# Banks of their own for the up rows, silu inside the attention, and the last down passes by token quarters, each with its final layer norm

## The chip, the cores and the metric

The kernel runs on one core of one Trainium2 chip. The metric is the device time of one execution in microseconds (us). The engines are TensorE (PE, with PEld for its weight loads), VectorE (DVE), ScalarE (ACT), GpSimd (POOL) and SyncE (SP, which here issues the DMAs). Each runs its own instruction list in order; they meet by semaphores (`wait_ge` and `then_inc`).

## The reference

One layer of a hybrid encoder, 1024 tokens by 1024 channels in float32:

- `h = x @ w_in`, whose columns feed three mixers: a pooling mixer; a state-space mixer (SSD), where `xbc = silu(conv4(xbc))` and the output is gated by `silu(z)`; and stick-breaking attention with 6 heads of 64, in blocks of 128 queries.
- `x1 = LN(alpha*x + concat(mixers) @ w_out)`.
- `up = conv3(x1 @ w_up)` with 2 x 2816 columns, `ffn = (silu(gate) * val) @ w_down`.
- `out = LN(alpha*x1 + ffn + sigmoid(x1 @ w_gate) * (p @ w_proj))`.

## The kernel before, in words

Everything is float32; products that matter for accuracy are made of three float32r matmuls: high x high, high x low and low x high, where a high part is the value rounded by ScalarE (`hi`, `op_hi`, `h_high`) and the low part the difference, taken by VectorE (`lo`, `op_lo`, `h_low`). Activations lie channels by tokens, in 8 tiles of 128 channels. The 8 PSUM banks of 128 x 512 float32 are shared out by hand. All orders are written out by hand, one list for each engine.

**Attention stage.** A grid of 92 ticks (`NTICK + LAG`) interleaves on all engines the attention of three head pairs (scores, two sigmoids on ScalarE, a scan and a multiplication on VectorE, transposes, a copy `weights_t` by ScalarE, the products with v) with the remaining input projection. `BY_STEP` spreads the pieces of the projection over the ticks. For seven tiles of the SSD input (`x0` to `C1`) the 4-tap conv is done here: `CONV_AT` is the tick of ScalarE's first tap into `cv`, `TAPS_AT` those of VectorE's three further taps (L1562). The tile with dt goes through exp and ln at tick 68 (L1208 to L1213). In the last tick ScalarE waits for the conv and does the silu of `x0`, `x1`, `x2` (L1218 to L1221), then all engines meet at a barrier (`meet`, L451). GpSimd has nothing to do in this stage.

**SSD.** After the barrier TensorE transposes the x and B tiles (`xt`, `bt`, L804) while ScalarE does the silu of B, C and z (L1230 to L1238). VectorE makes `x_dt`, copies the attention's output and runs the states (L1635, L1636); GpSimd makes `x_weighted`, the pooling sums and low parts of the attention output.

**FFN.** Eleven chunks (c = 0 to 10) of two up tiles pairs (pp = 0 even, 1 odd), each with a gate row (r = 0) and a value row (r = 1) of 128 x 1024. A pair of rows is computed by one level of a Strassen-like scheme: seven products (`A11, S1, S2, S3, A12, S4, A22`) of 12 matmuls with 512 columns each (L1009 to L1011), joined by five `combine` steps on VectorE (L1791 to L1801). Row r of tile pp lies in two PSUM banks (`up_row`): `X_BANK = (4, 2)` for r = 0 and `Y_BANK = 0` for r = 1 of both tiles. So the next tile's S2 and S3 may start only when the row before is read: `row_done` is counted by VectorE's second tap (L1767). A row is read by ScalarE's tap (L1343) and two VectorE taps (L1764, L1767); then silu, `glu` (L1774), and h in high and low parts.

The down product of chunk c - 1 runs as 16 `down` steps of 6 matmuls (L667 to L669) between `even` and `even_last` of chunk c. Each writes one of `DOWN_BANKS = (6, 7, 2, 3)` and is added to `acc` by `add_down` (L1816); down k waits for the addition of down k - 3 - 1. The loop order on TensorE is `even(c)`, 16 downs, `even_last(c)`, `odd(c)`. The weights of the down product come through one raw buffer `down_raw`, two loads at a time: D0A with D1A, then D0B with D1B, each after the low part before (L617).

**The end.** In the last chunk all 14 products are made first, then 16 downs for the first tile pair (pp = 0, which are chunk 9's h), then 16 for pp = 1 (the last chunk's h), ordered by halves of the tokens (`h = k // 8`). After half of the tokens is complete, `turn_back(m)` transposes token tile m back between downs; four tiles follow after the last down. A tile's norm: statistics on VectorE (L1701 to L1704), square root on ScalarE (L1462), reciprocal and product (L1949, L1950), normalisation on ScalarE (L1466), gain and bias on GpSimd (L2064, L2065) or, for the tiles in `GAIN_ON_VECTOR`, gain on VectorE (L1939), the last one's bias too (L1955); then a store.

Of the kernel before, what the change touches and what calls it, by code (L numbers as in the profile page):

```python
# [26 lines left out]
P = 128  # L27
D = 1024
S = 1024
HALF = 512  # L30
# [171 lines left out]

CONV_AT, TAPS_AT = [], []
# [6 lines left out]
GAIN_ON_VECTOR = (3, 5, 6, 7)  # L210
# [10 lines left out]
X_BANK, Y_BANK = (4, 2), 0  # L221
DOWN_BANKS = (6, 7, 2, 3)
# [50 lines left out]
def build(nc, ctx, a, out):  # L273
# [95 lines left out]
    h2l = [over("last_h_lo%d" % i, [P, S], (22, 24)[i], F32R) for i in range(2)]  # L369
    pu = over("partial", [P, 2, HALF], 8)  # L370
# [22 lines left out]
    def param(name, i=0, n=1):  # L393
# [21 lines left out]
    tap_done, conv_done, silu_done = sem("tap_done"), sem("conv_done"), sem("silu_done")  # L415
# [156 lines left out]
    def _(eng):  # L572
# [89 lines left out]
    def _(eng):  # L662
# [319 lines left out]
        def first_up(t):  # L982

            n = FFN0 + t
            dst, slot = up_row(t // 2, t % 2), RING_OF[n] % RINGS
            if t == 1:
                eng.wait_ge(sig_done, KT)
            elif t == 2:
                eng.wait_ge(u_free, 2 * KT)
            elif t == 3:  # L990
                eng.wait_ge(row_done, 2)
                column_tile(dst, slot, n, (1,)).then_inc(n1_read, 1)
            column_tile(dst, slot, n, (0,) if t == 3 else (0, 1)).then_inc(u_full, 1)

        def product(c, o, pp, it=0):

            first, second = slice(0, HALF), slice(HALF, S)
            x, y = X_BANK[pp], Y_BANK
# [15 lines left out]
        def down(c, k, pp, it=0):  # L1014

            j, h = (k // 2, k % 2) if pp == 0 else (k % 8, k // 8)
            s_, jc = slice(h * HALF, (h + 1) * HALF), slice(j % 4 * P, (j % 4 + 1) * P)
            if k == 0:
                eng.wait_ge(h_done, 2 * (c + pp) + 2 * it)
            if (pp == 0 and k % 8 == 0) or (pp == 1 and k in (0, 4)):  # L1020
                eng.wait_ge(op_lo_done, lo_count(c, D1A if j < 4 else D1B, pp) + 18 * it)
            first = 16 * (c - 1 + pp)
            if k >= 4 or pp:
                eng.wait_ge(dn_added, first + k - 3 + 16 * it)
            bank = 4 + k % 4 if c == LASTC else DOWN_BANKS[k % 4]
            h_h, h_l = (h2h, h2l) if pp else (hh, hl)
            for i in range(2):
                o = ((D0A, D1A), (D0B, D1B))[j // 4][i]
                last = three(ps[:, bank, :], op_place(c, o, pp, False)[:, jc], op_place(c, o, pp, True)[:, jc],
                             h_h[i][:, s_], h_l[i][:, s_], i == 0, i == 1)  # L1030
            last.then_inc(dn_full, 1)

        def even(c, it=0):
# [4 lines left out]
            eng.wait_ge(row_done, 4 * (c - 1) + 4 + 4 * it)  # L1038
# [16 lines left out]
        def odd(c, it=0):  # L1055
# [9 lines left out]
            eng.wait_ge(row_done, 4 * c + 2 + 4 * it)  # L1065
# [9 lines left out]
        def chunk(c, it=0):  # L1075

            even(c, it)
            for k in range(16):
                if k == 2:
                    eng.wait_ge(row_done, 4 * (c - 1) + 3 + 4 * it)  # L1080
                down(c, k, 0, it)
# [3 lines left out]
        def turn_back(m):  # L1085

            if m in (0, MT // 2):
                eng.wait_ge(dn_added, 16 * (CHUNKS - 1) + 8 + 8 * (m // 4))
# [4 lines left out]
            for kt in range(KT):  # L1093
                last = turn(two(m % 2)[:, kt * P:(kt + 1) * P], acc[:, kt, m * P:(m + 1) * P])
# [11 lines left out]
        eng.wait_ge(row_done, 4 * LASTC + 1)  # L1106
        for k in range(16):
            down(LASTC, k, 0)
        for k in range(16):
            if k in (9, 10, 12, 13):  # L1110
                turn_back((9, 10, 12, 13).index(k))
            down(LASTC, k, 1)
        for m in range(MT // 2, MT):
# [4 lines left out]
    def _(eng):  # L1118
# [57 lines left out]
        for n in range(NTICK + LAG):  # L1176
# [23 lines left out]
            if n in CONV_AT:  # L1200
# [3 lines left out]
                if j:  # L1204
                    eng.wait_ge(conv_done, j)
                act(cv[:, j, :], ht[:, j, :], ACT.Identity, scale=param("conv_w", 4 * j + 3),
                    bias=param("conv_b", j)).then_inc(tap_done, 1)
            if n == DT_AT + 1:  # L1208
# [9 lines left out]
            if n == NTICK + LAG - 1:  # L1218
                eng.wait_ge(conv_done, 7)
                for j in range(3):  # L1220
                    act(cv[:, j, :], cv[:, j, :], ACT.Silu).then_inc(silu_done, 1)  # L1221
# [8 lines left out]
        for j in (3, 4):  # L1230
            act(cv[:, j, :], cv[:, j, :], ACT.Silu).then_inc(silu_done, 1)
# [3 lines left out]
        for j in (5, 6):  # L1235
            act(cv[:, j, :], cv[:, j, :], ACT.Silu).then_inc(silu_done, 1)
        for j in range(3):
            act(ht[:, 7 + j, :], ht[:, 7 + j, :], ACT.Silu).then_inc(silu_done, 1)  # L1238
# [18 lines left out]
        nc.scalar.preload_act_table_set("natural_log_exp_and_others")  # L1257
# [198 lines left out]
        h_high(c, 1)  # L1456
        op_hi(c, D0B, 1)
        op_hi(c, D1B, 1)

        for m in range(MT):  # L1460
            eng.wait_ge(o_eps, m + 1)
            act(st[:, m, 15:16], st[:, m, 14:15], ACT.Sqrt).then_inc(o_sqrt, 1)  # L1462
            eng.wait_ge(o_aff, m + 1)
            if m >= 4:
                eng.wait_ge(stored[m % 4], 16 * (m // 4))
            act(on[:, m % 4, :], two(m % 2), ACT.Identity, scale=st[:, m, 13:14],  # L1466
# [4 lines left out]
    def _(eng):  # L1471
# [310 lines left out]
        def combine(c, pp, step, it=0):  # L1782

            n = 10 * (c - 1) + 5 * pp
            x, y = X_BANK[pp], Y_BANK
# [18 lines left out]
        def add_down(c, pp, ks, it=0):  # L1804

            first = 16 * (c - 1 + pp)
            for k in ks:
                j, h = (k // 2, k % 2) if pp == 0 else (k % 8, k // 8)
# [6 lines left out]
                bank = 4 + k % 4 if c == LASTC else DOWN_BANKS[k % 4]  # L1815
                v.tensor_tensor(dst, dst, ps[:, bank, :], ALU.add).then_inc(dn_added, 1)  # L1816
# [28 lines left out]
        def chunk(c, it=0):  # L1845
# [13 lines left out]
            add_down(c, 0, range(8, 16), it)  # L1859
# [72 lines left out]
        add_down(c, 1, range(9))  # L1932
# [4 lines left out]
        def gain(m):  # L1937
            eng.wait_ge(o_nrm, m + 1)
            v.tensor_tensor(on[:, m % 4, :], on[:, m % 4, :], lng[:, :], ALU.mult).then_inc(o_gain, 1)  # L1939

        for m in range(MT):
            eng.wait_ge(o_full, m + 1)
            statistics(m, two(m % 2)).then_inc(o_eps, 1)
            if m < 4:
                add_down(c, 1, ((9,), (10, 11), (12, 13), (14, 15))[m])
            if m - 1 in GAIN_ON_VECTOR:
                gain(m - 1)
            eng.wait_ge(o_sqrt, m + 1)
            link(v.reciprocal(st[:, m, 13:14], st[:, m, 15:16]))  # L1949
            v.scalar_tensor_tensor(out=st[:, m, 12:13], in0=st[:, m, 12:13], scalar=-1.0, in1=st[:, m, 13:14],  # L1950
                                   op0=ALU.mult, op1=ALU.mult).then_inc(o_aff, 1)
        m = MT - 1
        gain(m)
        eng.wait_ge(o_gain, len(GAIN_ON_VECTOR))
        v.tensor_tensor(on[:, m % 4, :], on[:, m % 4, :], lnb[:, :], ALU.add).then_inc(o_last, 1)  # L1955
# [3 lines left out]
    def _(eng):  # L1959
# [16 lines left out]

        meet(eng, 1)
# [165 lines left out]
```

## Time and profile before

| | us |
|---|---|
| median of 3 runs (1435.45 to 1437.79) | 1437.26 |
| the profiled execution | 1435.54 |
| its span in the trace | 1433.8 |
| TensorE busy | 1320.9 (92%) |
| VectorE busy | 879.5 (61%) |
| ScalarE busy | 507.4 (35%) |
| GpSimd busy | 208.1 (15%) |

The span runs from the first to the last instruction. Matmuls are drawn 0.40 us long, but they overlap: the next begins before one has ended, so TensorE's busy time leaves the pipeline's fill out. In a timeline row the bracket at the end gives the time that the engine stood idle before it and who released it. A row with x2 or more is several like instructions drawn as one, from the first one's start to the last one's end.

### The profile page before, as it was taken

Reading aid. Unit: us, or ns where it says so; the run is one execution under the profiler, and the core shown is the slowest. Engines: PE = TensorE matmul, PEld = TensorE weight load, DVE = VectorE, ACT = ScalarE, POOL = GpSimd, SP = SyncE. Lnnn points to the kernel's source line nnn. Section 1 sums busy time; section 2 is a strip of 40 time slices with the busy share of each in tenths; the row PEclk is TensorE's granted clock in tenths of the full one; section 3 lists DMA queues with packets and bytes.
Section 4 is the critical chain, followed back from the end, with each engine's and each line's share of the span. In section 5 each row is a group of like instructions: output and inputs, shape, how many; then the busy total and the mean of one; then the engine's idle time right before and its main releaser. Section 6 shows DMA issues by size and latency. Waiting matters only on the chain.

```text
span 1433.8 us, 16333 instructions
## 1 busy us (share of the span) xinstructions
PE 1320.9 (92%) x6084; PEld 1057.1 (74%) x6084; DVE 879.5 (61%) x1060; ACT 507.4 (35%) x747; POOL 208.1 (15%) x141
## 2 busy tenths in 40 slices
PE   7999999899767999999999999999999999999993
PEld 5787788677655788788877777777777777777772
DVE  3536646534387845532467676767676776767778
ACT  4445445444544224312333232423232332323412
POOL 0000000000271000510012111111122021111116
PEclk9999999899988999999999999999999999999996
DMA  5101000000001311310020111102010101111102
GB/s 217 52 23 45 30 30 30 30 30 15 1 1 59 103 44 60 102 45 30 30 74 30 60 44 44 59 31 83 32 59 29 59 29 59 44 45 59 59 16 117
DMA packets 22947, 71.93 MB, mean 50 GB/s; under 512 B 2544, under 2 KB 2800, under 8 KB 22896
## 3 DMA queue, kind: packets, MB, share of 16 engines
q1 hardware_dynamic: 22896, 71.22, 14.6%
q8 instruction: 36, 0.59, 0.2%
q14 instruction: 15, 0.12, 0.0%
HBM read 67.02 MB, written 4.19 MB: 50 GB/s over the span
## 4 chain that ended last, share of the span: by engine, by line
PE 59%; DVE 18%; ACT 5%; issue 5%; DMA 1%; ACTq 1%; POOL 1%; DVEq 0%; SPq 0%; POOLq 0%
PE ps L667 12%; PE ps L669 12%; PE ps L668 12%; PE ps L1009 5%; PE ps L1011 5%; PE ps L1010 5%; DVE conv_ff L1764 4%; DVE conv_ff L1767 2%; PE ps L761 2%; ACT conv_ff L1343 2%; DVE w_lo L553 1%; PE ps L721 1%; PE ps L745 1%; PE ps L804 1%; ACT w_hi L548 1%
## 5 line engine op out<-in xcount | busy, mean ns | idle before, releaser
L1816 DVE TENSOR_TENSOR acc<-acc,ps 128x512 f32<-128x512 f32 x176 | 117.6, 685 | 71.2 <-PE ps L669 71.2
L667 PE MATMUL ps<-x_hi,w_hi 128*128 128x512 f32 x336 | 142.0, 423 | 14.1 <-DVE x_lo L502 10.5
L667 PE MATMUL ps<-h_hi,w_hi 128*128 128x512 f32 x320 | 127.6, 399 | 11.3 <-DVE acc L1816 11.3
L668 PE MATMUL ps<-x_lo,w_hi 128*128 128x512 f32 x336 | 134.6, 400 | 0.0
L669 PE MATMUL ps<-x_hi,w_lo 128*128 128x512 f32 x336 | 134.2, 399 | 0.0
L669 PE MATMUL ps<-h_hi,w_lo 128*128 128x512 f32 x320 | 126.6, 396 | 0.0
L668 PE MATMUL ps<-h_lo,w_hi 128*128 128x512 f32 x320 | 126.6, 396 | 0.0
L1009 PE MATMUL ps<-mix_hi,w_hi 128*128 128x512 f32 x320 | 126.6, 396 | 0.0
L1010 PE MATMUL ps<-mix_lo,w_hi 128*128 128x512 f32 x320 | 126.6, 396 | 0.0
L1011 PE MATMUL ps<-mix_hi,w_lo 128*128 128x512 f32 x320 | 126.6, 396 | 0.0
L1009 PE MATMUL ps<-t_hi,w_hi 128*128 128x512 f32 x240 | 96.8, 403 | 18.2 <-DVE conv_ff L1767 18.2
L2039 POOL TENSOR_TENSOR weight_sums<-raw 128x512 f32<-128x512 f32 x20 | 30.4, 1518 | 495.4 <-DMA raw<-u_up 470.3
L548 ACT ACTIVATE w_hi<-weight_sums 128x512 fp32r<-128x512 f32 x40 | 25.3, 632 | 214.2 <-PE ps L669 170.9
L1011 PE MATMUL ps<-t_hi,w_lo 128*128 128x512 f32 x240 | 94.9, 396 | 0.0
L1010 PE MATMUL ps<-t_lo,w_hi 128*128 128x512 f32 x240 | 94.9, 395 | 0.0
L1343 ACT ACTIVATE conv_ff<-ps,params 128x1024 f32<-128x1024 f32 x44 | 53.1, 1206 | 103.6 <-DVE ps L1801 42.5
L1531 DVE TENSOR_TENSOR_SCAN ps<-ps,zero 128x1024 f32<-128x1024 f32 (+7 forms) x48 | 65.3, 1361 | 37.6 <-ACT ps L1167 37.5
L667 PEld LDWEIGHTS ps<-x_hi,w_hi 128*128 128x128 f32 x336 | 64.5, 192 | 28.5 <-DVE x_lo L502 10.5
L667 PEld LDWEIGHTS ps<-h_hi,w_hi 128*128 128x128 f32 x320 | 60.1, 188 | 29.7 <-DVE acc L1816 15.6
L667 PE MATMUL ps<-mix_hi,w_hi 128*128 128x512 f32 x192 | 76.9, 400 | 3.7 <-DVE mix_lo L1710 3.7
L1764 DVE SCALAR_TENSOR_TENSOR conv_ff<-ps,params,conv_ff 128x1023 f32<-128x1023 f32 x44 | 56.3, 1280 | 35.8 <-ACT conv_ff L1343 35.6
L1187 ACT ACTIVATE weights_t<-ps 128x512 f32<-128x512 f32 (+1 forms) x60 | 33.3, 555 | 122.9 <-PE ps L745 122.8
(240 smaller groups left out, 2847.9 us busy)
## 6 DMA issues: line engine op xcount, KB each, us to landing
raw<-u_up SPq DMA_DIRECT2D x44, 512.0 KB, 3.3
raw<-u_in SPq DMA_DIRECT2D x22, 512.0 KB, 3.3
down_raw<-u_down SPq DMA_DIRECT2D x44, 256.0 KB, 2.8
x_stage<-u_x SPq DMA_DIRECT2D x8, 512.0 KB, 7.7
raw<-u_out SPq DMA_DIRECT2D x8, 512.0 KB, 3.2
x_nat<-x_nat SPq DMA_DIRECT2D x8, 512.0 KB, 3.3
raw<-u_gate SPq DMA_DIRECT2D x8, 512.0 KB, 3.3
out<-o_norm SPq DMA_DIRECT2D x8, 512.0 KB, 2.6
```

The lines of the kernel that those rows point to most:

```text
L548: nc.scalar.activation(op_place(c, o, pp, False), op_raw(o), ACT.Copy).then_inc(op_hi_done, 1)
L667: mm(dst, w_hi, x_hi, start=first, stop=False)
L668: mm(dst, w_hi, x_lo, start=False, stop=False)
L669: return mm(dst, w_lo, x_hi, start=False, stop=last)
L1009: mm(dst, w_h[:, k], t_h[:, kt, :], start=fresh and kt == 0, stop=False, skip_group_check=True)
L1010: mm(dst, w_h[:, k], t_l[:, kt, :], start=False, stop=False, skip_group_check=True)
L1011: last = mm(dst, w_l[:, k], t_h[:, kt, :], start=False, stop=kt == 3, skip_group_check=True)
L1187: act(pair(un[:, :]), pair(ps[:, 6, :]), ACT.Copy).then_inc(wt_out, 1)
L1343: act(cf[:, r, :], up_row(pp, r), ACT.Identity, scale=column(w, 12, it), bias=column(b, 4, it)).then_inc(row_tap, 1)
L1531: link(v.tensor_tensor_scan(z[:, ::-1], z[:, ::-1], zero[:, 0:1].broadcast_to([P, keys]), 1.0, ALU.mult, ALU.add))
L1764: v.scalar_tensor_tensor(out=cf[:, r, 1:], in0=src[:, :S - 1], scalar=column(w + 1, 12, it), in1=cf[:, r, 1:], op0=ALU.mult, op1=ALU.add). ...
L1816: v.tensor_tensor(dst, dst, ps[:, bank, :], ALU.add).then_inc(dn_added, 1)
```

## The change

- `Y_BANK` becomes `(0, 6)`: row 1 of the odd tile goes to banks 6 and 7. The waits of S2 move: even S2 waits for `row_done` 4(c-1) + 2, odd S2 for none (in the last chunk for the chunk before); down 0 waits for the odd tile's row 1.
- In a chunk VectorE does the taps and five down additions before `op_lo(A11, 1)`.
- In the attention, three taps after a conv tile's start, ScalarE takes the sigmoid of the conv (`GATE_AT`) and GpSimd multiplies it on; the z tiles follow the same way. The ten silus on ScalarE go. A tile's first tap waits for the silu of the one before, and comes at the earliest 3 ticks (`GATE_LAG`) after its last tap.
- The last down passes: four quarters of 256 tokens; matmuls have 256 columns instead of 512, all four terms (two pp, two i) accumulate in one bank, which holds two channel tiles (`LAST_BANKS`), and VectorE adds once for both. In the first quarter the terms go in three phases by when h is ready. Each later quarter carries the transposes of two tiles of the quarter before. Weights D0B, D1B of pp = 1 get places of their own.
- Norm: reciprocal and a `tensor_scalar` instead of `scalar_tensor_tensor`; tiles 0 to 5 by ScalarE and GpSimd, tiles 6 and 7 by two `scalar_tensor_tensor` on VectorE.

```diff
-    CONV_AT.append(max([evacuated_at(("tile", _name)) + 1] + [t[-1] + 1 for t in TAPS_AT[-1:]]))
+    CONV_AT.append(max([evacuated_at(("tile", _name)) + 1] + [t[-1] + GATE_LAG for t in TAPS_AT[-1:]]))
+GATE_AT = [t[-1] + 1 for t in TAPS_AT]
+for _name in H_TILES[7:10]:
+    GATE_AT.append(max(evacuated_at(("tile", _name)) + 1, GATE_AT[-1] + 2))
-X_BANK, Y_BANK = (4, 2), 0
-DOWN_BANKS = (6, 7, 2, 3)
+X_BANK, Y_BANK = (4, 2), (0, 6)
+DOWN_BANKS, LAST_BANKS = (6, 7, 2, 3), (4, 5, 0, 1)
...
+        def last_down(q, jp, k):
+            pp, i = divmod(k, 2)
+            h_h, h_l = (h2h, h2l) if pp else (hh, hl)
+            s_ = slice(q * QUARTER, (q + 1) * QUARTER)
+            for j in (2 * jp, 2 * jp + 1):
+                o = ((D0A, D1A), (D0B, D1B))[j // 4][i]
+                w_h, w_l = op_place(LASTC, o, pp, False), op_place(LASTC, o, pp, True)
+                jc = slice(j % 4 * P, (j % 4 + 1) * P)
+                dst = ps[:, LAST_BANKS[jp], j % 2 * QUARTER:(j % 2 + 1) * QUARTER]
+                mm(dst, w_h[:, jc], h_h[i][:, s_], start=k == 0 and j % 2 == 0, stop=False, skip_group_check=True)
+                mm(dst, w_h[:, jc], h_l[i][:, s_], start=False, stop=False, skip_group_check=True)
+                last = mm(dst, w_l[:, jc], h_h[i][:, s_], start=False, stop=k == 3, skip_group_check=True)
+            if k == 3:
+                last.then_inc(dn_full, 1)
...
-            eng.wait_ge(row_done, 4 * (c - 1) + 4 + 4 * it)
+            eng.wait_ge(row_done, 4 * (c - 1) + 2 + 4 * it)
...
-            eng.wait_ge(row_done, 4 * c + 2 + 4 * it)
+            if c == LASTC:
+                eng.wait_ge(row_done, 4 * (c - 1) + 4)
...
-                if k == 2:
-                    eng.wait_ge(row_done, 4 * (c - 1) + 3 + 4 * it)
+                if k == 0:
+                    eng.wait_ge(row_done, 4 * (c - 1) + 4 + 4 * it)
...
+        for jp in range(4):
+            if jp in (0, 2):
+                eng.wait_ge(op_lo_done, lo_count(LASTC, D1B if jp else D1A, 0))
+            last_down(0, jp, 0)
+            last_down(0, jp, 1)
+        eng.wait_ge(h_done, 2 * LASTC + 1)
+        for jp in range(4):
+            if jp in (0, 2):
+                eng.wait_ge(op_lo_done, lo_count(LASTC, D1B if jp else D1A, 1))
+            last_down(0, jp, 2)
+        eng.wait_ge(h_done, 2 * LASTC + 2)
+        for jp in range(4):
+            last_down(0, jp, 3)
+        for q in range(1, 4):
+            for jp in range(4):
+                eng.wait_ge(dn_added, 16 * (LASTC - 1) + 4 * (q - 1) + jp + 1)
+                for k in range(4):
+                    last_down(q, jp, k)
+                if jp in (0, 2):
+                    turn_back(2 * q - 2 + jp // 2)
+        for m in range(MT - 2, MT):
+            turn_back(m)
...
+            if n in GATE_AT:
+                j = GATE_AT.index(n)
+                if j < 7:
+                    eng.wait_ge(conv_done, j + 1)
+                    act(ht[:, j, :], cv[:, j, :], ACT.Sigmoid).then_inc(gate_done, 1)
+                else:
+                    for hh_ in range(2):
+                        wait_evacuated(eng, PLACE[(H_TILES[j], hh_)])
+                    eng.wait_ge(silu_done, j)
+                    act(ht[:, 6, :], ht[:, j, :], ACT.Sigmoid).then_inc(gate_done, 1)
...
             combine(c, 0, 4, it)
+            taps(c, 0, 0, it)
+            add_down(c, range(5), it)
             op_lo(c, A11, 1, it)
-            taps(c, 0, 0, it)
-            add_down(c, 0, range(8), it)
+            add_down(c, range(5, 8), it)
...
-        add_down(c, 0, range(0, 2))
-        taps(c, 1, 1)
         op_lo(c, D0A, 1)
         op_lo(c, D1A, 1)
-        add_down(c, 0, range(2, 6))
+        taps(c, 1, 1)
         glu(c, 1)
-        add_down(c, 0, range(6, 9))
-        h_low(c, 1)
-        add_down(c, 0, range(9, 11))
         op_lo(c, D0B, 1)
         op_lo(c, D1B, 1)
-        add_down(c, 0, range(11, 16))
-        add_down(c, 1, range(9))
+        h_low(c, 1)
+        add_last(0, range(4))
...
+        for j in range(10):
+            eng.wait_ge(gate_done, j + 1)
+            x = cv[:, j, :] if j < 7 else ht[:, j, :]
+            g.tensor_tensor(x, x, ht[:, min(j, 6), :], ALU.mult).then_inc(silu_done, 1)
```

## Rows read from the trace of the kernel before

**Rows 1.** The page, part 1: busy us, share of the span, instructions.

```profile
PE 1320.9 (92%) x6084; PEld 1057.1 (74%) x6084; DVE 879.5 (61%) x1060; ACT 507.4 (35%) x747; POOL 208.1 (15%) x141
```

**Rows 2.** Waits of TensorE: us in total, times, longest.

```profile
PE ps L1009 <- DVE conv_ff L1767: 18.2, 19, 1.9
...
PE ps L667 <- DVE acc L1816: 11.3, 10, 1.2
```

**Rows 3.** Timeline of TensorE, one loop chunk: start, us, instruction, count, [idle before].

```profile
943.00 0.50 PE L667 MATMUL ps<-h_hi,w_hi 128*128 128x512 f32 x1 [1.19 <-DVE acc L1816]
...
968.99 0.49 PE L1009 MATMUL ps<-t_hi,w_hi 128*128 128x512 f32 x1 [0.52 <-DVE conv_ff L1767]
969.32 0.39 PE L1010 MATMUL ps<-t_lo,w_hi 128*128 128x512 f32 x1
...
990.38 0.49 PE L1009 MATMUL ps<-t_hi,w_hi 128*128 128x512 f32 x1 [1.54 <-DVE conv_ff L1767]
```

**Rows 4.** Timeline of all engines around the barrier after the attention.

```profile
375.18 0.60 ACT L1136 ACTIVATE h_tiles<-ps 128x512 f32<-128x512 f32 x1 [0.64 <-PE ps L669]
...
380.18 7.07 PE L804 MATMUL ps<-tables,conv 128*128 128x128 f32 x40 [5.04 <-ACTq L451]
...
396.63 7.79 POOL L2006 TENSOR_TENSOR mix_lo<-sb_out,mix_hi 128x1024 fp32r<-128x1024 f32 x3
```

**Rows 5.** Timeline of the end, and the window around the stall at 576.84.

```profile
1352.85 0.40 PE L667 MATMUL ps<-h_hi,w_hi 128*128 128x512 f32 x1
...
1354.74 1.28 DVE L553 TENSOR_TENSOR w_lo<-down_raw,w_hi 128x512 fp32r<-128x512 f32 x2
...
1359.33 1.16 ACT L548 ACTIVATE w_hi<-down_raw 128x512 fp32r<-128x512 f32 x2 [1.46 <-DMA down_raw<-u_down]
...
1402.77 0.40 PE L669 MATMUL ps<-last_h_hi,w_lo 128*128 128x512 f32 x1
...
1406.08 0.68 DVE L1701 BATCH_NORM_STATS2 ln_stats<-ps 128x6 f32<-128x512 f32 x1
...
1407.71 1.93 DVE L1939 TENSOR_TENSOR o_norm<-o_norm,ln_gain 128x1024 f32<-128x1024 f32 x1
...
1429.41 1.22 DVE L1955 TENSOR_TENSOR o_norm<-o_norm,ln_bias 128x1024 f32<-128x1024 f32 x1
...
core 0: us, PE busy (x) PEld busy (x) DVE busy (x) ACT busy (x) POOL busy (x), PEclk, DMA share, GB/s
576.00:580.50 4.50, 3.66 (x10) 2.93 (x11) 4.50 (x3) 1.72 (x2) 4.42 (x3) 0.62 0.29 88
```

**Rows 6.** Timeline of VectorE in the same loop chunk and the next.

```profile
942.26 1.87 DVE L1816 TENSOR_TENSOR acc<-acc,ps 128x512 f32<-128x512 f32 x3
...
998.18 0.69 DVE L553 TENSOR_TENSOR w_lo<-down_raw,w_hi 128x512 fp32r<-128x512 f32 x1
...
1001.88 0.70 DVE L1799 TENSOR_TENSOR ps<-partial,ps 128x512 f32<-128x512 f32 x1 [1.44 <-PE ps L1011]
...
1005.27 1.28 DVE L1764 SCALAR_TENSOR_TENSOR conv_ff<-ps,params,conv_ff 128x1023 f32<-128x1023 f32 x1
...
1007.90 1.27 DVE L1816 TENSOR_TENSOR acc<-acc,ps 128x512 f32<-128x512 f32 x2
```

**Rows 7.** Timeline of ScalarE, the tap behind combine 4.

```profile
1002.91 1.21 ACT L1343 ACTIVATE conv_ff<-ps,params 128x1024 f32<-128x1024 f32 x1 [3.19 <-DVE ps L1799]
```

**Rows 8.** Timeline of the attention around tick 68.

```profile
286.24 1.26 ACT L1206 ACTIVATE conv<-h_tiles,params 128x1024 f32<-128x1024 f32 x1
...
303.42 0.92 PE L761 MATMUL ps<-weights_t,v_natural 128*128 128x256 f32 x3 [0.82 <-ACT weights_t L1187]
```

**Rows 9.** Timeline of short matmuls; the page's group of weight loads (busy, mean ns).

```profile
73.80 0.28 PE L721 MATMUL ps<-k_hi,q_hi 64*128 64x256 f32 x2
73.91 0.27 PE L721 MATMUL ps<-k_lo,q_hi 64*128 64x256 f32 x2
...
428.33 3.84 PE L860 MATMUL ps<-tables,small 128*128 128x128 f32 x32
...
L667 PEld LDWEIGHTS ps<-h_hi,w_hi 128*128 128x128 f32 x320 | 60.1, 188 | 29.7 <-DVE acc L1816 15.6
```

More of the change, by code:

```diff
@@ L508, in op_place @@
     def op_place(c, o, pp, lo):
+        if c == LASTC and pp and o in (D0B, D1B):
+            return (last_l if lo else last_h)[:, (D0B, D1B).index(o), :]
         s_ = (position(c, o, pp) + 4) % 6
@@ L533, in wait_op_place @@
         q = position(c, o, pp) - 6
+        if c == LASTC and pp and o in (D0B, D1B):
+            eng.wait_ge(prod_full, product_count(c, S2, 1))
+            return
         if c == 1 and q < 0:
@@ L1012, in product, with down @@
             last.then_inc(prod_full, 1)
-        def down(c, k, pp, it=0):
-            j, h = (k // 2, k % 2) if pp == 0 else (k % 8, k // 8)
+        def down(c, k, it=0):
+            j, h = k // 2, k % 2
             s_, jc = slice(h * HALF, (h + 1) * HALF), slice(j % 4 * P, (j % 4 + 1) * P)
             if k == 0:
[L1019 to L1026, printed above, removed]
+                eng.wait_ge(h_done, 2 * c + 2 * it)
+            if k % 8 == 0:
+                eng.wait_ge(op_lo_done, lo_count(c, D1A if j < 4 else D1B, 0) + 18 * it)
+            if k >= 4:
+                eng.wait_ge(dn_added, 16 * (c - 1) + k - 3 + 16 * it)
@@ L1105, in _ @@
         odd(LASTC)
[L1106 to L1113, printed above, removed]
+        eng.wait_ge(row_done, 4 * LASTC + 2)
+        eng.wait_ge(h_done, 2 * LASTC)
+        for jp in range(4):
[19 more added lines that the diff above has]
+        for m in range(MT - 2, MT):
             turn_back(m)
@@ L1228, in task @@
             return two(pair), d_free[pair]
-        for j in (3, 4):
-            act(cv[:, j, :], cv[:, j, :], ACT.Silu).then_inc(silu_done, 1)
+        nc.scalar.preload_act_table_set("natural_log_exp_and_others")
         for g in range(2):
@@ L1941, in _, with rows, affine @@
[L1941 to L1947, printed above, removed]
+        def rows(m):
+            return two((1, 3)[m % 2])
+        def affine(m):
             eng.wait_ge(o_sqrt, m + 1)
             link(v.reciprocal(st[:, m, 13:14], st[:, m, 15:16]))
-            v.scalar_tensor_tensor(out=st[:, m, 12:13], in0=st[:, m, 12:13], scalar=-1.0, in1=st[:, m, 13:14],
-                                   op0=ALU.mult, op1=ALU.mult).then_inc(o_aff, 1)
@@ L1952, in _ @@
[L1952 to L1955, printed above, removed]
+            v.tensor_scalar(st[:, m, 12:13], st[:, m, 12:13], st[:, m, 13:14], -1.0, ALU.mult,
+                            ALU.mult).then_inc(o_aff, 1)
+        for q in range(1, 4):
+            m = 2 * q - 2
+            add_last(q, (0,))
+            eng.wait_ge(o_full, m + 1)
+            statistics(m, rows(m)).then_inc(o_eps, 1)
+            add_last(q, (1,))
+            affine(m)
+            add_last(q, (2,))
+            eng.wait_ge(o_full, m + 2)
+            statistics(m + 1, rows(m + 1)).then_inc(o_eps, 1)
+            add_last(q, (3,))
+            affine(m + 1)
@@ new lines, in _ @@
+        for m in range(MT - 2, MT):
+            eng.wait_ge(o_full, m + 1)
+            statistics(m, rows(m)).then_inc(o_eps, 1)
+            eng.wait_ge(stored[m % 4], 16)
+            y = on[:, m % 4, :]
+            v.scalar_tensor_tensor(out=y, in0=rows(m), scalar=st[:, m, 12:13], in1=lng[:, :], op0=ALU.subtract,
+                                   op1=ALU.mult).then_inc(o_cent, 1)
+            eng.wait_ge(o_sqrt, m + 1)
+            link(v.reciprocal(st[:, m, 13:14], st[:, m, 15:16]))
+            eng.wait_ge(o_cent, m - MT + 3)
+            v.scalar_tensor_tensor(out=y, in0=y, scalar=st[:, m, 13:14], in1=lnb[:, :], op0=ALU.mult,
+                                   op1=ALU.add).then_inc(o_last, 1)
```

86 lines of the change are left out of this document (41 added, 45 removed).

## The prediction

> **What bounds the kernel now.** I read the page first, for busy shares: TensorE works 1320.9 of 1433.8 us and nothing else comes near [rows 1], so time can only leave in TensorE's idle stretches or at the ends, where it has nothing to do. Next the waits of TensorE: two of its largest are 18.2 us for the second tap of an up row, in 19 waits, and 11.3 us for the additions of down results, in 10 [rows 2]. The timeline of one loop chunk shows where they stand: before down 4 (943.00), before S2 of the odd tile (968.99) and before S2 of the even tile of the next chunk (990.38) [rows 3]. Last the two ends that the diff touches: from 375.14 to 380.18 TensorE waits for ScalarE, which loads a table and does three silus [rows 4]; and after the last down matmul at 1402.77 the program runs to 1433.8, 31 us of layer norm of the last tiles [rows 5].
>
> What one stall costs: idle plus restart. A matmul is drawn 0.40 long, the next one starts 0.233 after it, and only the second one after a stall comes 0.33 later (968.99 to 969.32) [rows 3]. So a stall costs its idle time + 0.17 + 0.10 = idle + 0.27. The 0.233: from 968.99 to 990.38 are 84 matmuls (seven products of 12), less 1.54 + 0.27 for the stall at the end: 19.58 / 84. A product is 2.8.
>
> **Chunks.** Row 1 of the odd tile gets banks 6 and 7 of its own. Both S2 products then wait for a row that has long been read, so all 19 stalls go: 18.2 + 19 x 0.27 = 23.3 [rows 2, 3]. Three of these waits come back at other places. Down 0 now waits for the odd tile's second tap (done by 990.38, wanted at 999): nothing. A11 and S1 of the odd tile write banks 2 and 3 as before. S2 of the odd tile writes bank 7, freed by down 13, which S1's wait for down 15 already covers: nothing.
>
> What is late next? The vector chain. The odd tile starts two products and a stall before 968.99, at 968.99 - 5.6 - 0.69 = 962.7 [rows 3]; from there to the downs TensorE has 13 products, 36.4, to 999.1. VectorE in that stretch does not wait for TensorE up to the low part of D1B at 998.18 [rows 6]; that and the low part of A22 are 0.69 each, so combine 4, which until now waited for TensorE until 1001.88, starts at about 999.5. From there the rows give: activation 1.03 after it (1002.91) [rows 7], 1.21 long, taps 0.15 later, two taps and the start of the additions 2.63 after (1005.27 to 1007.90) [rows 6], and the first addition releases down 4 after 0.74 (942.26 to 943.00) [rows 3, 6]. That is 999.5 + 1.03 + 1.21 + 0.15 + 2.63 + 0.74 = 1005.3. Down 4 is ready at 999.1 + 24 x 0.233 = 1004.7. So a stall of 0.6, 0.75 with its restart, is left where 1.19 + 0.27 = 1.46 is now. The low part of A11, moved from before the taps to behind five additions, is what keeps the taps at 1005.27 today, where the activation ends at 1004.12; in its new place it falls between additions that wait for TensorE, and its reader comes after all the downs: nothing. Nine chunks have this stall: 11.3 less the one in the last tile (0.9), plus 9 x 0.27, is 12.8; 9 x 0.75 = 6.8 stays; 6.0 goes. Chunks together: **-29.3**. Bounds: if the down stall stays whole, -23.3; if it vanishes, -36.
>
> **Silu in the attention.** ScalarE gets 10 sigmoids of 1.05 and loses 10 silus; GpSimd gets 10 multiplications of 128x1024, 2.6 each by the nearest row (three in 7.79) [rows 4]. No sigmoid adds a table load: the scores use the same function. The ScalarE queue behind a sigmoid holds the copies of transposed weights, which TensorE wants only a tick later. One place has no slack: the tap of tile C1 (1.26, at 286.24) moves from two ticks earlier into the tick with the softplus and its table loads, whose end TensorE already waits for (303.42) [rows 8]: +1.3. GpSimd's multiplications hold up VectorE where it reads two operands from SBUF: a gain multiplication begun at 1407.71 beside GpSimd took 1.93 instead of 1.22 [rows 5]. Only taps and low parts are of that kind in the attention; TensorE has little idle there, so nearly all is covered. I take +0.7 (bounds 0, and 10 x 0.7 = 7). Sum **+2.0**.
>
> **Between attention and scan.** The last evacuation ends at 375.78; the barrier can let TensorE go at 375.95 instead of 380.18 [rows 4]: -4.2. The 40 transposes behind it start at half clock after an idle of 5.04: they take 7.07, 0.18 each, where 32 matmuls of the same width take 3.84, 0.12 each, at full clock [rows 4, 9]. After an idle of under 1 us the clock should stay up; 34 of them stand before VectorE's last x dt: about 6.4 becomes 3.7, -2.7 (bounds 0 and -2.7). The later silus (C, z) stood beside VectorE's copies and states, which set the pace: 0. Sum **-6.9**.
>
> **The tail.** Call T the start of the downs (1352.85) [rows 5]. Now: T + 50.3 to the end of the downs, T + 81.0 to the end.
>
> 192 matmuls of 512 columns become 384 of 256. Their spacing is the greatest unknown. Rows: score matmuls of 256 columns follow at 0.11 to 0.12 (73.80, 73.91), though two share the array by rows; full 128x128 loads with a 128-column matmul each follow at 0.12 on average (3.84 / 32), without the first one's latency 0.11 [rows 9]. Half of 0.233 is 0.117: I take it, and 384 x 0.117 = 192 x 0.233 = 44.8, no change. Upper bound: a load is drawn 0.188 long [rows 9]; at that spacing 72.2, +27.4.
>
> Now the first quarter, which has too little work to cover the second tile's h. (1) k = 0, 1: 48 matmuls, 5.6; at half of it TensorE waits for the low part of D1B,0, ending at T + 3.2 (1354.74 + 1.28): end T + 6.1. (2) k = 2 needs D0A,1 and D1A,1: they land at T + 6.5 (1359.33) [rows 5], high 0.62, low 0.68 and 0.6: T + 8.5, a stall of 2.4. Its second half needs D1B,1, whose load is issued only then (one raw buffer): landing 3.3 later as between 1356.02 and 1359.33, T + 11.8; high parts, low parts behind glu: T + 13.9. TensorE stood from T + 9.9, a stall of 4.0. End T + 15.4. (3) k = 3 needs h low, behind taps, glu, the low parts and ScalarE's high copy: T + 15.5. End T + 18.3.
>
> Each further quarter: 96 x 0.117 = 11.2, and two tiles of 8 transposes, 0.9 + 0.1 each: 13.2. Downs end at T + 18.3 + 39.6 = T + 57.9, 7.6 later than now. Four additions of 0.69 and two tiles' statistics and scalars (2.0 each) take VectorE 6.8 of each 13.2, two tiles' gain and bias GpSimd 4 x 2.6 = 10.4: covered.
>
> Behind it: last add and transposes 2.2; statistics 1.6 (1406.08 to 1407.71) [rows 5]; centring with gain 1.3, reciprocal 0.2, scale with bias 1.2; and this once more, 4.3 each; the store's 3.2 (from 1430.63 to the end, 1433.8) [rows 5]: 14.0. Tile 5's bias on GpSimd (2.6) lies over tile 6's last step, which reads SBUF twice: up to +2. End T + 57.9 + 16 = T + 73.9: -7.0. But two stalls of 2.4 and 4.0 may halve the clock: after an idle of 3.65 the granted clock of 576 to 580.5 was 0.62 [rows 5], a loss of some 1.5; I add 1.0. Sum **-6.0**, bounds -11 and 0 without the spacing.
>
> **Sum.** -29.3 + 2.0 - 6.9 - 6.0 = -40.2 on the profiled execution's 1435.5 (span 1433.8): 1395.3. The median of the timed runs, 1437.3, is 1.7 above; so 1397.
>
> **Rivals.** (a) Weight loads bind the short matmuls (0.15 to 0.19 apart). For: loads are drawn 0.188 long, and each begins when the matmul before begins. Against: 0.11 with 128 columns, where loads are drawn as long. 1397 + 27 = 1424; from 0.15, 1410. Chance 6%. (b) Loads don't overlap at all with a matmul on the same rows: 0.188 + 0.117 = 0.305, 384 x 0.305 = 117, +72: 1469, **slower**; it turns into a loss from (44.8 + 40.2) / 384 = 0.22. Against: then 512 columns would be 0.40 apart, not 0.233. Chance 2%. By the Trainium skill ("TensorE: Matmul & The Clock Gate", Part 3, The mechanism), LDWEIGHTS overlaps with in-flight matmuls only when the row group differs; by that rule (b) would hold, and the trace's 0.233 and 0.11 speak against it. (c) GpSimd's products and late gates hold VectorE or ScalarE in the attention: ten waits for a whole multiplication, 26 at most, 1405 to 1421. For: ScalarE already lets TensorE wait there [rows 8]. Chance 8%. (d) The chunk change does less than it says: VectorE's chain is nearer than I counted and gives the stalls back at down 4 or at S4, half of 29: 1411. For: combine 4 has no slack left. Against: VectorE is idle 39% [rows 1]. Chance 12%. The forecast: 72%.
>
> **Numbers.** Own range of the forecast 1390 to 1405; with (c), (d) and part of (a): 1389 to 1411. A measurement here tells 0.2% from no change. Faster by more: 0.95 (all but (b) and what I have not thought of), within 0.2% 0.02, slower 0.03.
>
> **What would show it.** Right: no wait on L1767's taps before S2; a stall under 1 us at down 4; transposes 0.11 apart after the barrier, some 4 us earlier; 256-column matmuls 0.117 apart; in the first quarter two stalls of 2 to 4 us; the end 16 us behind the last down. Wrong: a spacing over 0.13, attention more than 5 us longer, or chunks over 63 us (14 products, 96 matmuls of downs and the stall are 39.2 + 22.4 + 0.75 = 62.4).

## The result, and the profile after

| | median us | runs | ratio to before, 95% interval |
|---|---|---|---|
| before | 1436.36 | 4 (1433.75 to 1437.79) | |
| changed | 1392.76 | 4 (1391.88 to 1394.17) | 0.9699 [0.9682, 0.9717] |

The forecast was 1397 (1389 to 1411). The profiled execution of the changed kernel took 1391.88, its span is 1389.8. The page, part 1, as in [rows 1]: TensorE has 192 matmuls more (the last downs have 256 columns) and 9.6 us less busy time; GpSimd has the ten products.

```profile
PE 1311.3 (94%) x6276; PEld 1064.6 (77%) x6276; DVE 860.7 (62%) x1041; ACT 502.4 (36%) x744; POOL 233.2 (17%) x152
```

Waits of TensorE after (us in total, times, longest), to be held against [rows 2]: the wait for the second tap of an up row is gone, that for the down additions has shrunk to 1.5; the one for the transposed weights of the attention has grown from 0.8 to 1.9 (L771); and new ones stand before the last downs (L1049).

```profile
PE ps L1049 <- DVE last_w_lo L563: 5.7, 1, 5.7
...
PE ps L1049 <- DVE w_lo L563: 2.7, 2, 2.5
...
PE ps L771 <- ACT weights_t L1225: 1.9, 1, 1.9
...
PE ps L677 <- DVE acc L1855: 1.5, 7, 0.2
```

Timeline after: the wait behind the softplus tick, as in [rows 8], and TensorE's restart behind the barrier with VectorE's first states operation, as in [rows 4].

```profile
303.59 1.13 PE L771 MATMUL ps<-weights_t,v_natural 128*128 128x256 f32 x4 [1.95 <-ACT weights_t L1225]
...
376.22 4.59 PE L814 MATMUL ps<-tables,conv 128*128 128x128 f32 x40 [0.72 <-ACTq L456]
...
385.65 0.55 DVE L1675 TENSOR_TENSOR states<-states,small 128x384 f32<-128x384 f32 x1
```

The end, TensorE, as in [rows 5]. T, the start of the last downs, is 1312.17:

```profile
1312.17 0.28 PE L1049 MATMUL ps<-h_hi,w_hi 128*128 128x256 f32 x1
...
1315.39 0.39 PE L1049 MATMUL ps<-h_hi,w_hi 128*128 128x256 f32 x1 [0.22 <-DVE w_lo L563]
...
1320.94 0.36 PE L1049 MATMUL ps<-last_h_hi,w_hi 128*128 128x256 f32 x1 [2.45 <-DVE w_lo L563]
...
1328.26 0.58 PE L1049 MATMUL ps<-last_h_hi,last_w_hi 128*128 128x256 f32 x1 [5.67 <-DVE last_w_lo L563]
...
1373.94 0.28 PE L1051 MATMUL ps<-last_h_hi,last_w_lo 128*128 128x256 f32 x1
```

Three anchors cut both spans into parts: the last projection matmul before the barrier (374.75 before, 375.10 after), the restart before the FFN (576.84; 568.81), and T (1352.85; 1312.17).

| part | before | after | change | forecast |
|---|---|---|---|---|
| start to barrier | 374.75 | 375.10 | +0.35 | +2.0 |
| barrier, scan, output projection | 202.09 | 193.71 | -8.4 | -6.9 |
| FFN up to T | 776.01 | 743.36 | -32.65 | -29.3 |
| T to the end | 80.95 | 77.6 | -3.3 | -6.0 |

(The attention started 0.6 earlier in this execution, at 60.94 instead of 61.56, so its own part is +0.97.) The measured median is 4.2 below the forecast. In the table the gains that I had set too low (attention, barrier, chunks: 1.7 + 1.5 + 3.3) outweigh the one that I had set too high (the end, 2.7); that errors of both signs met is luck.

### The profile page after: what moved, and what is told of

Read it like the earlier page. It is cut to its first block, busy times and chain, and to the rows that moved or that the text cites. A ratio compares the mean times of both kernels' runs of the same rounds, so it can differ in the third digit from the quotient of the medians.

```text
span 1389.8 us, 16699 instructions
## 1 busy us (share of the span) xinstructions
PE 1311.3 (94%) x6276; PEld 1064.6 (77%) x6276; DVE 860.7 (62%) x1041; ACT 502.4 (36%) x744; POOL 233.2 (17%) x152
## 4 chain that ended last, share of the span: by engine, by line
PE 68%; DVE 12%; ACT 4%; issue 3%; DMA 2%; DVEq 0%; SPq 0%; ACTq 0%
PE ps L677 12%; PE ps L679 12%; PE ps L678 12%; PE ps L1020 7%; PE ps L1018 7%; PE ps L1019 7%; PE ps L771 2%; DMA down_raw<-u_down 2%; DVE conv_ff L1804 1%; ACT conv_ff L1381 1%; PE ps L731 1%; PE ps L755 1%; PE ps L814 1%; DVE w_lo L563 1%; PE ps L1049 1%
## 5 line engine op out<-in xcount | busy, mean ns | idle before, releaser
L1855 DVE TENSOR_TENSOR acc<-acc,ps 128x512 f32<-128x512 f32 x144 | 96.1, 685 | 53.4 <-PE ps L679 52.9
L1019 PE MATMUL ps<-mix_lo,w_hi 128*128 128x512 f32 x320 | 126.6, 396 | 0.0
L1020 PE MATMUL ps<-mix_hi,w_lo 128*128 128x512 f32 x320 | 126.6, 396 | 0.0
L677 PE MATMUL ps<-h_hi,w_hi 128*128 128x512 f32 x288 | 114.6, 398 | 1.5 <-DVE acc L1855 1.5
L679 PE MATMUL ps<-h_hi,w_lo 128*128 128x512 f32 x288 | 113.9, 396 | 0.0
L678 PE MATMUL ps<-h_lo,w_hi 128*128 128x512 f32 x288 | 113.9, 395 | 0.0
L679 PE MATMUL ps<-mix_hi,w_lo 128*128 128x512 f32 x192 | 76.4, 398 | 0.0
L678 PE MATMUL ps<-mix_lo,w_hi 128*128 128x512 f32 x192 | 76.4, 398 | 0.0
```

The costliest lines, as they stand in the source:

```text
L677: mm(dst, w_hi, x_hi, start=first, stop=False)
L678: mm(dst, w_hi, x_lo, start=False, stop=False)
L679: return mm(dst, w_lo, x_hi, start=False, stop=last)
L1019: mm(dst, w_h[:, k], t_l[:, kt, :], start=False, stop=False, skip_group_check=True)
L1020: last = mm(dst, w_l[:, k], t_h[:, kt, :], start=False, stop=kt == 3, skip_group_check=True)
L1855: v.tensor_tensor(dst, dst, ps[:, DOWN_BANKS[k % 4], :], ALU.add).then_inc(dn_added, 1)
```

## Experiments

Nine kernels, called by their numbers below (kernel 4 is that of experiment 4). The first four ran beside the kernel before at 1435.74 us (median of 11 runs), the next four beside it at 1435.36, the last at 1434.95.

**1. The banks alone.** Kernel before with the second bank pair, its waits and VectorE's order in the chunk.

```diff
-X_BANK, Y_BANK = (4, 2), 0
+X_BANK, Y_BANK = (4, 2), (0, 6)
...
-            op_lo(c, A11, 1, it)
             taps(c, 0, 0, it)
-            add_down(c, 0, range(8), it)
+            add_down(c, 0, range(5), it)
+            op_lo(c, A11, 1, it)
+            add_down(c, 0, range(5, 8), it)
```

> Kernel before with the second bank pair for row 1 of the odd tile, its waits and VectorE's new order in the chunk; attention and the end as before (downs of the last chunk in banks 4, 5, 0, 1, the transposes back in 2, 3, 6, 7). Theory: all of the 32.7 us by which the stretch from TensorE's restart before the FFN to the first last down is shorter in the changed kernel comes from this part: 32 to 33 less than before, about 1404; no wait for L1767's taps, the downs' stall 0.2 idle. Rival, the prediction's count: 29.3 less, 1407. Rival: some of it came only with the new end, because the last chunk's VectorE order is another: 23 to 27 less.

Measured: 1403.19, ratio 0.9771 [0.9758, 0.9784], 32.5 less. Its waits for down additions come to this, from 11.3 in [rows 2]; none is left for the up row's tap:

```profile
PE ps L667 <- DVE acc L1816: 2.4, 8, 0.9
```

From the restart before the FFN to T it takes 743.7, the changed kernel 743.4. So the whole gain of the FFN stretch is this edit's; the new end has no part in it.

**2. Silu in the attention alone.** The `GATE_AT`, ScalarE and GpSimd hunks on the kernel before.

> Kernel before with the silus moved into the attention, nothing else. Theory from the two traces: -4.3 of waiting at the barrier, -2.7 because the 40 transposes run at the full granted clock, about -1.5 behind them, +1.0 in the attention: 7 to 8.5 less than before, about 1428.5. Rival, the prediction's sum: GpSimd's products cost the attention 2.0 and nothing is gained behind the transposes: 4.9 less, 1431.5.

Measured: 1428.77, ratio 0.9955 [0.9941, 0.9969], 7.0 less (4.5 to 8.5 by the interval). The median stands at the lower end of the theory's 7 to 8.5, and the interval doesn't exclude the prediction's 4.9; the trace is plainer than the total. TensorE's 40 transposes start after 0.72 instead of 5.04 and take 4.59 instead of 7.07 [rows 4]:

```profile
378.00 4.59 PE L808 MATMUL ps<-tables,conv 128*128 128x128 f32 x40 [0.72 <-ACTq L455]
```

**3. Both, with the old end.**

> The two parts above together, the end as before. Theory: they add, and the new end is worth 3.3 in the changed kernel: this one takes 3.3 more than the changed kernel, about 1396. Rival: the new end is worth the predicted 6.0 and the rest less: 1399. Rival: the parts share stalls and don't add: more than 1400.

Measured: 1396.91, ratio 0.9726 [0.9714, 0.9739]. 38.8 less, where the two parts alone give 39.5: they add. The changed kernel at 0.9699 is 0.0027 lower, about 4 us, the intervals just meeting; by the traces the end is worth 3.3 (T to the end 81.0 in this kernel, 77.6 in the changed one).

**4. Why the end gave so little: raw buffers of their own.** Changed kernel; D0B and D1B of both tiles load early into two places (the norm's gain and bias follow into them later), so no down load waits for another's low part. The edit also changes two orders in the last chunk: each of ScalarE's two taps of the last tile stands behind the high copies that it was ahead of, the silu behind the second tap, and VectorE takes the first tile's low parts of D0B and D1B before combine 4. What it gives belongs to the places and the orders together.

```diff
+    dn_own = [over("down_own%d" % i, [P, 2, HALF], 11 + i) for i in range(2)]
...
+        for pp in range(2):
+            for i in range(2):
+                eng.dma_start(dn_own[pp][:, i, :], a["u_down"][2 * (LASTC - 1 + pp) + i][:, HALF:D]
+                              ).then_inc(own_in[pp], 16)
```

> Changed kernel, with raw buffers of their own for the weights D0B, D1B of both tiles in the last chunk (loaded as soon as the slots are free; the norm's gain and bias come into the same slots afterwards), so that no down load waits for another's low part. Theory: the stalls of 2.45 and 5.67 us in the first token quarter are a chain of loads through one raw buffer, and the lower clock behind them is theirs too. Left is about 2 us before the second half of k = 2 (low part of D1B behind glu) and under 0.5 before k = 3: first quarter 7 to 8.5 shorter, in all 1385 (1383 to 1387). Rival: h, not the weights, sets the quarter's end (taps, glu and h_low would end at the same time anyway): 2 to 3 less, 1390. Rival: the extra megabyte of loads beside the last products slows VectorE and ScalarE: no gain.

Measured: 1385.60, ratio 0.9651 [0.9638, 0.9663]; T to the end 70.0 instead of 77.6. Of three waits in the first quarter one of 1.79 is left, at the place expected:

```profile
1324.52 0.38 PE L1059 MATMUL ps<-last_h_hi,last_w_hi 128*128 128x256 f32 x1 [1.79 <-DVE last_w_lo L571]
```

In the changed kernel's trace the chain of loads is what the wait of 5.67 hangs on: TensorE waits for VectorE's low part, that for ScalarE's high part, and ScalarE stands 6.26 us for the last load. That the whole 7.6 comes from this chain isn't shown, because of the orders changed with it.

```profile
1318.84 1.15 ACT L558 ACTIVATE w_hi<-down_raw 128x512 fp32r<-128x512 f32 x2 [1.65 <-DMA down_raw<-u_down]
1326.25 1.15 ACT L558 ACTIVATE last_w_hi<-down_raw 128x512 fp32r<-128x512 f32 x2 [6.26 <-DMA down_raw<-u_down]
```

**5. Is it the banks or the order?** Changed kernel with VectorE's old order in the loop (low part of A11, taps, eight additions).

> Changed kernel, but in the loop VectorE takes the low part of A11 of the odd tile before the taps again, as the kernel before did. Theory: the reorder is what took the stall at down 4 from 1.2 to 0.2 idle in each chunk: the taps end 0.6 to 0.7 later, so the stall comes back as 0.7 to 0.9 idle in nine chunks, 5 to 7 us in all, some 1398. Rival: the banks alone did it, because combine 4 no longer waits: stall still 0.2 idle, time as the changed kernel's.

Measured: 1400.72 in one run, and 10.0 us of waits for down additions in 9 (longest 1.3) instead of 1.5 in 7. The kernel before has 10.3 in the same nine chunks: at down 4 the banks alone give next to nothing. The price is more than the theory's 0.7 for each chunk. VectorE in one chunk of this kernel, and of the changed one:

```profile
857.36 0.69 DVE L1839 TENSOR_TENSOR ps<-partial,ps 128x512 f32<-128x512 f32 x1
860.13 0.69 DVE L563 TENSOR_TENSOR w_lo<-raw,w_hi 128x512 fp32r<-128x512 f32 x1 [2.08 <-ACT w_hi L558]
860.74 1.28 DVE L1804 SCALAR_TENSOR_TENSOR conv_ff<-ps,params,conv_ff 128x1023 f32<-128x1023 f32 x1
```

```profile
855.90 0.69 DVE L1839 TENSOR_TENSOR ps<-partial,ps 128x512 f32<-128x512 f32 x1
858.28 1.28 DVE L1804 SCALAR_TENSOR_TENSOR conv_ff<-ps,params,conv_ff 128x1023 f32<-128x1023 f32 x1 [1.69 <-ACT conv_ff L1381]
```

From combine 4 to the tap it is 3.38 against 2.38. The low part itself is 0.6 of that; 0.4 more is its wait for the high part, which ScalarE makes only behind its own tap.

**6. An idle before the transposes.** Changed kernel with four copies on ScalarE ahead of the barrier.

```diff
+        eng.wait_ge(silu_done, 10)
+        for k in range(4):
+            act(ht[:, 6, :], ht[:, 6, :], ACT.Copy).then_inc(pad, 1)
+            eng.wait_ge(pad, k + 1)
         meet(eng, 1)
```

> Changed kernel with four more copies of 128x1024 on ScalarE ahead of the barrier after the attention (they change nothing in the result). Theory: TensorE waits 4.2 to 4.9 us longer there, and the 40 transposes behind it run at the lower clock level again, 0.18 instead of 0.11 apart: up to 2.7 more, so that the first states operation behind them comes 6 to 7.5 later. Rival: the transposes were slow before because of the silus that ran beside them, not because of the idle time ahead: only 4.2 to 4.9 later, transposes 0.11 apart.

Measured: 1398.37 in one run. The transposes begin 4.1 later than in the changed kernel, and run at the lower of the two clock levels first; window rows of this kernel, then of the changed one (us, busy time and count of each engine, PEclk, DMA share, GB/s):

```profile
380.00:384.00 4.00, 3.65 (x18) 3.65 (x19) 1.88 (x4) 1.54 (x2) 1.75 (x3) 0.57 0.00 0
384.00:388.00 4.00, 4.00 (x33) 3.90 (x32) 2.18 (x6) 1.94 (x2) 3.23 (x5) 1.00 0.00 0
```

```profile
376.00:380.00 4.00, 3.78 (x35) 3.78 (x36) 1.95 (x4) 2.75 (x4) 2.48 (x4) 1.00 0.00 0
```

In the first window 18 have begun, in the changed kernel's 35; they take 6.25 in all against 4.59, with no silu beside them in either. The first states operation follows 5.5 later than in the changed kernel (391.18, 385.65), under the 6 expected: the slow part cost 1.4 this time, where the kernel before lost 2.2, because the clock rose sooner. Idle time as the cause is shown, its size varies.

**7. Twice the products on GpSimd.** The second product of each pair changes the result; it took 1.9 to 2.9 us beside the first one's 2.4.

```diff
             g.tensor_tensor(x, x, ht[:, min(j, 6), :], ALU.mult).then_inc(silu_done, 1)
+            eng.wait_ge(silu_done, j + 1)
+            g.tensor_tensor(x, x, x, ALU.mult)
```

> Changed kernel in which GpSimd multiplies each of the ten products in the attention once more by itself (this changes the result). Theory from the trace: GpSimd's products cost VectorE next to nothing there, because VectorE has slack for what they hold up: attention up to 1 us longer. Rival, the prediction's 0.07 for each of ten products (0.7 in all) and its bound (0.7 for each): 0.7 to 7 more, to be seen as longer taps (1.28 alone) with TensorE waiting behind them.

Measured: 1392.13 in one run; from TensorE's matmul at 285 to the transposes 90.9 as in the changed kernel. The twelve taps of the window from 200 to 377 are as long as in the kernel before, 1278 ns (line, busy us, mean ns):

```profile
L1602 DVE SCALAR_TENSOR_TENSOR conv<-h_tiles,params,conv 128x1023 f32<-128x1023 f32 (+2 forms) x12 | 15.3, 1279 | 0.2
```

**8. Filling the first quarter; the end reordered.** On kernel 4.

```diff
-DOWN_BANKS, LAST_BANKS = (6, 7, 2, 3), (4, 5, 0, 1)
+DOWN_BANKS, LAST_BANKS = (6, 7, 2, 3), ((4, 5, 0, 1), (2, 3, 6, 7))
...
+        last_down(0, 0, 2)
+        last_down(0, 1, 2)
+        eng.wait_ge(row_done, 4 * LASTC + 3)
+        for k in range(3):
+            last_down(1, 0, k)
+        eng.wait_ge(op_lo_done, lo_count(LASTC, D0B, 1))
+        last_down(0, 2, 2)
+        last_down(0, 3, 2)
...
                                    op1=ALU.mult).then_inc(o_cent, 1)
+        for m in range(MT - 2, MT):
+            y = on[:, m % 4, :]
             eng.wait_ge(o_sqrt, m + 1)
```

> Changed kernel with the own raw buffers of the run before, and two things more: (1) the quarters take banks 4, 5, 0, 1 and 2, 3, 6, 7 in turn, so that the first three terms of the second quarter's first tile pair stand in the first quarter before its last term, and term k = 2 waits only for the weights that it reads; (2) at the end VectorE centres both last tiles before it scales the first, so that no operation with two SBUF inputs stands beside GpSimd's last one. Theory: (1) takes away the 1.8 us stall in the first quarter and the lower clock behind it (60 matmuls 0.146 apart instead of 0.120, 1.6): 3.4 less; (2) the scaling of tile 6 takes 1.28 instead of 3.27: 1.5 to 2 less. From 1385.6 to 1380.5 (1379.5 to 1382). Rival: the clock falls anyway, at another place: 1382. Rival for (2): the two last stores now follow each other closely and take longer: 0 to 0.5 less from it.

Measured: 1378.99, ratio 0.9604 [0.9588, 0.9620]: 6.6 less than kernel 4, and the fastest with kernel 9. From T (1313.15) to the end 64.6. TensorE waits nowhere in the first quarter and keeps the full clock:

```profile
1313.00:1331.00 18.00, 18.00 (x154) 17.95 (x153) 14.06 (x17) 6.19 (x8) 0.00 (x0) 1.00 0.10 40
```

At the end VectorE centres tile 7 before it scales tile 6. The scaling was held 2 us by GpSimd in the changed kernel:

```profile
1379.01 2.34 POOL L2128 TENSOR_TENSOR o_norm<-o_norm,ln_bias 128x1024 f32<-128x1024 f32 x1
1379.16 3.27 DVE L2016 SCALAR_TENSOR_TENSOR o_norm<-o_norm,ln_stats,ln_bias 128x1024 f32<-128x1024 f32 x1
...
1385.36 1.28 DVE L2016 SCALAR_TENSOR_TENSOR o_norm<-o_norm,ln_stats,ln_bias 128x1024 f32<-128x1024 f32 x1
```

and stands behind it here (POOL's last ends at 1371.2):

```profile
1368.88 2.34 POOL L2148 TENSOR_TENSOR o_norm<-o_norm,ln_bias 128x1024 f32<-128x1024 f32 x1
...
1371.85 1.28 DVE L2036 SCALAR_TENSOR_TENSOR o_norm<-o_norm,ln_stats,ln_bias 128x1024 f32<-128x1024 f32 x1
```

From the last down to the end 13.9 instead of 15.9: the 2.0 in full. From T to the end it is 5.4 less than in kernel 4, and 6.6 lie between the medians; ahead of T the edit changes nothing, so the other 1.2 isn't its doing.

**9. C1's tap two ticks later.** On kernel 8.

> The run before (filled) with the first tap of tile C1 two ticks later, out of the tick in which ScalarE computes softplus with its table loads (the three other taps and the gates behind it follow). Theory: the tap is what lengthens TensorE's wait for the transposed weights from 0.82 to 1.95: the wait goes back to 0.8, and with it the lower clock that followed it in some executions: 1.1 to 2 less, about 1377.6. Rival: the tap only moves the wait, since the ticks behind are as full: same time, a new wait of about 1 us at the later tick. Rival: C1's gate, the last of the seven, now comes too late for z and the barrier: 1 to 3 more.

Measured: 1378.96, ratio 0.9608 [0.9594, 0.9621]: the same as kernel 8. The wait is back at its old length, and no other came:

```profile
302.94 1.13 PE L784 MATMUL ps<-weights_t,v_natural 128*128 128x256 f32 x4 [0.82 <-ACT weights_t L1244]
```

From 285.83 to the transposes it is 89.2, 1.7 less than the changed kernel's 90.9. The rest of the execution took this back (0.5 each before, in the scan stage and behind it), which is what executions differ by. The local gain is shown, one in the median is not.

## Why the prediction was right, step by step

**The pieces of a stall.** Idle + 0.27 held: 19 waits gone are 23.3, the down waits fell from 11.3 + 10 x 0.27 = 14.0 to 1.5 + 7 x 0.27 = 3.4. The 0.9 + 0.27 of the last tile's wait lay behind T before; without it the two sums are 23.3 + 12.8 - 3.4 = 32.7, and 32.65 was measured.

**Down 4: the mis-sized term (6.0, measured 9.4).** The mechanism was right, the moved low part too. I left 0.6 idle in each of nine chunks; it was 0.2 in seven. Combine 4 starts 0.2 behind the first down (855.90 and 855.69), where I had 0.4; and the rest is my own double count: the 0.6 was the delay against the point where the next matmul would have started, so 0.17 of the restart was in it already.

```profile
861.65 0.50 PE L677 MATMUL ps<-h_hi,w_hi 128*128 128x512 f32 x1 [0.20 <-DVE acc L1855]
```

A whole chunk takes 62.1 (first down to first down, 855.69 to 917.76), where I had 62.4.

**Attention (2.0, measured 0.97 in one execution).** The tap in the tick of the softplus costs 1.95 - 0.82 = 1.13, close to the 1.3. The 0.7 for GpSimd was not there: the taps kept their length, VectorE's low parts of this stretch grew from 1225 to 1289 ns, and nothing waited for them; experiment 7 doubles GpSimd's work without effect. The 0.97 is a kind value: from TensorE's restart at 61.56 (60.94 after) to the last projection matmul it took 313.2 before and 314.2 in the changed kernel, but 316.6 and 316.7 in kernels 3 and 4, with the same instructions, so the cost was 1 to 3.5 by the clock's course (last section).

**Barrier (4.2, measured 4.3) and clock (2.7, measured 2.2)** up to the first states operation: 11.65 behind the transposes' start before, 9.43 after. Another 1.8 came behind it, which I had put at 0. Experiment 6 keeps ScalarE free of the silus and still has the idle: from its first states matmul (394.62) to the restart before the FFN it takes 180.7, the kernel before 181.6 (from 395.28), the changed one 179.7. The clock's course was worth little there: over the 26 us behind that matmul kernels 2 and 8 have a granted clock of 0.76 and the changed one 0.86, yet they take 179.9 and the changed one 179.7. The silus of C and z in ScalarE's queue are what the kernel before alone has; but kernel 6 doesn't have them and takes 0.9 more than the changed one, so how the 1.8 divides stays open.

**The tail: the step that was too good (6.0, measured 3.3).** Point by point from T = 1312.17:
- k = 0, 1 end at T + 6.1 by the forecast; the last of its 48 starts at T + 6.05. D1A's low part was put at T + 8.5 and TensorE restarts at T + 8.8.
- D1B's low part was put at T + 13.9, from a landing 3.3 after the low part before. It came 5.45 after (1320.80 to 1326.25), and TensorE restarted at T + 16.1: 2.2 lost. I took one row (1356.02 to 1359.33) as the price of every load of the kind. In the kernel before the next load's landing was hidden, as ScalarE was not waiting for it.
- A wait of 5.67 halved the clock: the next 36 matmuls took 6.44 instead of 4.2, 2.2 lost where I had allowed 1.0.

```profile
1328.00:1331.00 3.00, 2.74 (x13) 2.74 (x14) 1.44 (x2) 1.63 (x2) 0.00 (x0) 0.50 0.00 0
```

- Each further quarter was put at 13.2 and took 13.1 (turn to turn). The spacing: 0.118 in a run of one kind, 0.120 in the later quarters, against 0.117; rivals (a) and (b) are out. By the Trainium skill ("TensorE: Matmul & The Clock Gate", Part 3, The mechanism) a load overlaps only with matmuls of another row group; these all use the full array, and 256 columns follow at 0.118, so the trace does not agree with that rule. The same section of the Trainium skill also has loads into the background weight buffer pulled ahead of running matmuls; the 0.118 would fit that.
- The end behind the last down was put at 16, GpSimd's hold on tile 6 with it: 15.9.

Rival (c) gave nothing here, as experiment 7 shows, and (d) was wrong in sign: the chunks gave more than I said.

## What to carry to other kernels

Where one buffer serves a chain of loads, price the chain's last link from the slowest landing that can be seen, and first ask whether a place free by then could take the load earlier; here that, with the orders changed beside it, was worth 7.6 where the whole new end had given 3.3. When a stall in front of dense matmuls can be filled with work that is due anyway, the clock behind it is won as well. A low part or another small operation ahead of a critical one costs its own time and its own wait: look at what its input is queued behind.

## What the runs showed of the hardware that I had not expected

**The same wait, two courses of the clock.** Eight of the kernels have the wait of 1.94 to 1.95 at about 304. It was followed by the full clock in six of them, the changed one among these, and by less in kernels 4 and 3, whose instructions in the attention are the same. Windows of the changed kernel, then of kernel 4:

```profile
305.00:320.00 15.00, 15.00 (x80) 12.26 (x79) 2.85 (x3) 6.93 (x10) 1.79 (x1) 1.00 0.11 37
```

```profile
305.00:320.00 15.00, 15.00 (x68) 12.16 (x67) 3.25 (x3) 5.85 (x9) 0.00 (x0) 0.90 0.11 37
```

80 matmuls against 68; the way from this wait to the first states matmul is 85.5 in the one and 87.2 in the other. From this wait to the last projection matmul it is 71.5 in each of the six and 73.2 in the two. The two had already a slower course behind the wait before it (2.39, at 285): 19.6 from there to this restart, where the six have 18.2 to 18.5. Behind the wait of 1.79 in kernel 4 (1324.52) the clock was 0.72 in the 6 us from 1324. So a stall near 2 us costs its length and sometimes 1.6 more.

**The last load is slow every time.** In the four kernels that keep the changed kernel's loads, ScalarE waits 6.12 to 6.26 for it. It takes 5.4 where the one before takes 3.5, and both move 512 KB. The trace shows what the landing waits for: in the changed kernel all but nine packets are through by 1324.0, and these pass one by one up to 1326, with a mean busy share of 0.06 at most, about one of the 16 DMA engines. In each of the four the queue that the page calls "instruction" moves one packet of some 16 KB at the end of the load, just before this rest; in the kernel before it comes after the load. That this packet holds the last nine up fits all of these traces, but no run moves it, so the cause stays open.

**GpSimd holds VectorE for the whole rest of its operation.** The scaling above began 0.15 after GpSimd's and ended 1.1 after GpSimd's end: it stood still rather than shared. The kernel before shows the same in small: its product of one column (L1950) took 2.33 when begun 0.03 behind a GpSimd operation of 2.34 (1409.75 and 1409.72), and 0.16 at its shortest. By the Trainium skill ("SBUF — State Buffer", SBUF: two separate sides) the port pair is an exclusive lock, taken by whoever starts first, and a VectorE operation with two SBUF inputs needs it; the 3.27 agrees with that. The centring, whose other input is in PSUM, took 1.28 beside GpSimd (1377.78, GpSimd from 1376.59 to 1378.93).
